# Token halves across the seam between the second mixer and the second MLP, with a multiply moved to GpSimd

## What is computed

```python
h = rms_norm(x, mix_norm_pre)
m = hybrid_mixer(h, ...)                  # ends in concat([attn, rec]) @ w_out
x = x + rms_norm(m, mix_norm_post)        # root over the 1024 features of m, per token
h = rms_norm(x, mlp_norm_pre)
a = relu(h @ w_ff_in)                     # 1024 -> 4096
x = x + rms_norm((a * a) @ w_ff_out, mlp_norm_post)
```

## Time and profile before

| | before |
|---|---|
| median of three executions | 1423.48 us |
| profiled execution, time | 1422.14 us |
| profiled execution, span | 1420.3 us |
| TensorE busy | 1398.5 us, 98% |
| ScalarE busy | 832.2 us, 59% |
| VectorE busy | 698.4 us, 49% |
| GpSimd busy | 202.0 us, 14% |
| granted TensorE clock | 0.999 of full |

### The profile page before, as it was taken

How to read it: one execution, slowest core, us unless ns; L and a number is a source line. 1 busy time by engine, 2 the same in 40 slices (tenths; PEclk the granted TensorE clock), 3 DMA queues, 4 the chain that set the end, 5 groups by cost and what they waited for, 6 DMA issues and landing times.

```text
span 1420.3 us, 18417 instructions
## 1 busy us (share of the span) xinstructions
PE 1398.5 (98%) x6734; PEld 1121.1 (79%) x6734; DVE 698.4 (49%) x1228; ACT 832.2 (59%) x1174; POOL 202.0 (14%) x236
## 2 busy tenths in 40 slices
PE   7999999999999999999999999999999999999998
PEld 5887877777778888888888887777788888888887
DVE  6992477877734455544154165757465301213324
ACT  7536566776755656665365477645756655535442
POOL 1210100100111111111111111010101111111111
PEclk9999999999999999999999999999999999999999
DMA  9996966566579888888878997754667898888873
GB/s 298 221 188 154 233 156 141 132 156 142 115 197 220 193 188 193 187 202 192 214 177 187 214 233 158 160 139 108 145 153 162 193 202 192 190 202 180 206 163 89
DMA packets 82692, 254.76 MB, mean 179 GB/s; under 512 B 16816, under 2 KB 20016, under 8 KB 82608
## 3 DMA queue, kind: packets, MB, share of 16 engines
q0 software_dynamic: 32400, 117.98, 46.2%
q1 hardware_dynamic: 48768, 132.50, 30.9%
q10 hardware_dynamic: 1440, 3.15, 0.6%
HBM read 128.03 MB, written 3.41 MB: 93 GB/s over the span
## 4 chain that ended last, share of the span: by engine, by line
PE 94%; DVE 3%; ACT 2%; issue 0%; DMA 0%; DVEq 0%; ACTq 0%
PE pg L559 27%; PE pg L561 27%; PE pg L560 27%; PE ps L733 2%; PE py L811 1%; PE ps L947 1%; PE ps L957 1%; ACT pairs_r L1241 1%; PE py L967 1%; DVE acc L1558 1%; PE ps L735 0%; ACT kq_raw L1242 0%; PE ps L949 0%; DVE acc L1555 0%; PE px L632 0%
## 5 line engine op out<-in xcount | busy, mean ns | idle before, releaser
L559 PE MATMUL pg<-x_hi,w_hi 128*128 128x512 f32 x1088 | 429.0, 394 | 0.0
L561 PE MATMUL pg<-x_hi,w_lo 128*128 128x512 f32 x1088 | 424.0, 390 | 0.0
L560 PE MATMUL pg<-x_lo,w_hi 128*128 128x512 f32 x1088 | 423.5, 389 | 0.0
L523 POOL DMA_DIRECT2D w_lo<-w_raw x225 | 194.0, 862 | 1186.3 <-ACT w_lo L1080 1134.9
L1079 ACT ACTIVATE w_hi<-w_raw 128x1024 fp32r<-128x1024 f32 x222 | 233.4, 1051 | 100.9 <-PE pg L561 99.8
L559 PEld LDWEIGHTS pg<-x_hi,w_hi 128*128 128x128 f32 x1088 | 204.3, 188 | 43.5 <-issue 1.6
L561 PEld LDWEIGHTS pg<-x_hi,w_lo 128*128 128x128 f32 x1088 | 204.2, 188 | 43.0
L560 PEld LDWEIGHTS pg<-x_lo,w_hi 128*128 128x128 f32 x1088 | 204.4, 188 | 42.5 <-issue 1.0
L1080 ACT ACTIVATE w_lo<-w_raw 128x1024 fp32r<-128x1024 f32 x222 | 232.3, 1046 | 0.0
L559 PE MATMUL pg<-act_hi,w_hi 128*128 128x512 f32 x424 | 165.0, 389 | 0.0
L561 PE MATMUL pg<-act_hi,w_lo 128*128 128x512 f32 x424 | 165.0, 389 | 0.0
(11 more groups left out here) (384 smaller groups left out, 1743.9 us busy)
## 6 DMA issues: line engine op xcount, KB each, us to landing
w_raw<-weights SPq DMA_DIRECT2D x226, 512.0 KB, 4.8
w_lo<-w_raw POOLq DMA_DIRECT2D x225, 512.0 KB, 5.7
kq_rot<-kq_raw SPq DMA_DIRECT2D x64, 64.0 KB, 3.3
hid<-x SPq DMA_DIRECT2D x4, 512.0 KB, 5.4
hid<-x ACTq DMA_DIRECT2D x8, 256.0 KB, 5.3
out<-hid SPq DMA_DIRECT2D x16, 128.0 KB, 1.8
u_dram<-hid SPq DMA_DIRECT2D x4, 256.0 KB, 5.4
pairs<-u_dram SPq DMA_DIRECT2D x8, 128.0 KB, 6.8
```

Of the source, the lines that this page charges most:

```text
L523: pool.dma_start(w_lo[:, s], w_raw[:, s], accum_op=ALU.add).then_inc(lo_in[s], 16)
L559: pe.matmul(bank[:], wh, xh(k), start=n == 0, stop=False)
L560: pe.matmul(bank[:], wh, xl(k), start=False, stop=False)
L561: last = pe.matmul(bank[:], wl, xh(k), start=False, stop=n == len(ks) - 1)
```

## The change

- **out2 6 and 7 in halves.** TensorE makes tokens 0 to 255 of both units, then tokens 256 to 511 of both. The four results go to four places (`mid_bank`). The sum of squares for half 0 is made inside the second half of out2 6.
- **ff 0, 1 and 2 in halves, no double products.** In each half ff 0 and ff 1 go side by side, tile of input by tile of input, so that one tile of input feeds 6 matmuls; then ff 2. The sum for half 1 lies inside the first half of ff 0 and 1.
- **The root is applied by GpSimd**, in place on `acc`, 16 multiplies of 128x256, between its DMA issues; VectorE then needs one instruction for each tile and half for the new residual.
- ScalarE's high parts, its evacuations and the weight copies for ff 2 are put in a new order. The relu of ff 0 to 2 is made in two halves each.

```diff
+            def scaled_by_root(half, tiles):
+                cols = halves[half]
+                pool.wait_ge(rstd_ready, 4 + half)
+                for k in tiles:
+                    pool.tensor_tensor(acc[:, k, cols], acc[:, k, cols], rstd[:, cols], ALU.mult).then_inc(mid_scaled, 1)
             for v in range(11, len(UNITS)):
+                if v == UNIT[("ff", 2)]:
+                    scaled_by_root(0, range(0, 3))
+                if v == UNIT[("ff", 3)]:
+                    scaled_by_root(0, range(3, KT))
+                    scaled_by_root(1, range(0, 4))
+                if v == UNIT[("ff", 4)]:
+                    scaled_by_root(1, range(4, KT))
                 lo(v, v % RING)
...
+            def last_outputs():
+                for half, cols in enumerate(halves):
+                    for m in (6, 7):
+                        s = UNIT[("out2", m)] % RING
+                        if half == 0:
+                            pe.wait_ge(lo_in[s], lows(UNIT[("out2", m)]))
+                            pe.wait_ge(pg_free[TILE[("out2", m)] % 2], TILE[("out2", m)] // 2)
+                        for k in range(KT):
+                            if (half, m) == (1, 6) and k in (1, 3):
+                                mid_sum(0, k // 2)
+                            last = half_products(mid_bank[m][half], s, k, mx2_hi, mx2_lo, cols)
+                        last.then_inc(tile_done if half else mid_full, 1)
+            def first_units():
+                slot = [UNIT[("ff", i)] % RING for i in range(3)]
+                for half, cols in enumerate(halves):
...
+                    for k in range(KT):
+                        if half == 0 and k in (1, 3):
+                            mid_sum(1, k // 2)
+                        pe.wait_ge(xlo_done, SPLIT["norm4"] + KT * half + k + 1)
+                        for i in range(2):
+                            last = half_products(ff_bank[i][half], slot[i], k, x_hi, x_lo, cols)
+                            if half == 1 and k == KT - 1:
+                                last.then_inc(tile_done, 1)
+                    if half == 0:
+                        pe.wait_ge(lo_in[slot[2]], lows(UNIT[("ff", 2)]))
+                        pe.wait_ge(mid_read, 1)
+                    for k in range(KT):
+                        last = half_products(ff_bank[2][half], slot[2], k, x_hi, x_lo, cols)
+                last.then_inc(tile_done, 1)
...
-            for m in range(KT):
+            for m in range(6):
                 ahead(("out2", m))
-                put(act.activation(x_hi[:, m], hid[:, m], ACT.Copy, scale=par("mlp_pre", m)), xhi_done)
                 a = done(("out2", m))
                 square(4, m, a)
-                put(act.activation(a5_hi[:, m], a, ACT.Copy, scale=both[:, m:m + 1]), xhi_done)
                 free(act.activation(acc[:, m], a, ACT.Copy), ("out2", m))
-            inverse_root(4, rstd)
+            ahead(("out2", 6))
+            mid_out(6, 0)
+            mid_out(7, 0)
+            mid_root(0, ("stat", 4))
+            mid_out(6, 1)
+            norm4_hi(0, 0)
+            u = UNIT[("out2", 7)] + RING - 1
+            act.wait_ge(w_landed[u % RING], 16 * (u // RING + 1))
+            act.wait_ge(tile_done, TILES_AFTER[u - RING])
+            act.activation(w_hi[:, u % RING], w_raw[:, u % RING], ACT.Copy)
+            norm4_hi(0, 1)
+            put(act.activation(w_lo[:, u % RING], w_raw[:, u % RING], ACT.Copy, scale=-1.0), hi_done)
+            norm4_hi(0, 2)
+            mid_out(7, 1)
+            norm4_hi(0, 3)
+            norm4_hi(0, 4)
+            mid_root(1, ("stat4", 1))
+            for k in range(5, KT):
+                norm4_hi(0, k)
             ahead(("ff", 0))
...
+            def norm4_res(half, k):
+                cols = halves[half]
+                dve.wait_ge(mid_scaled, KT * half + k + 1)
+                put(stt(hid[:, k, cols], acc[:, k, cols], par("mix_post", k), hid[:, k, cols], ALU.mult, ALU.add), res_done)
...
+            for half in range(2):
+                for k in range(KT):
+                    norm4_res(half, k)
+                    if k > 0:
+                        norm4_lo(half, k - 1)
+                    if (half, k) == (0, 1):
+                        mid_added(1)
+                norm4_lo(half, KT - 1)
```

## The result

The changed kernel takes 1427.16 us (median of 7 runs, 1426.32 to 1429.21) against 1423.30 us before (7 runs, 1423.08 to 1425.09): a ratio of 1.0029 with an interval of 1.0020 to 1.0038. That is 3.9 us slower where 0.8 us faster was forecast. The profiled execution has 1426.55 us and a span of 1424.4 us.

A forecast was written before the change was run, and what follows sets the result against it. TensorE, busy 98% of the span, was taken to bound the kernel. Work -9.3, stalls +3.2, +0.4 and +2.0 gave -3.7; code loading +3.0 made it -0.7 us: median 1422.7 us, range 1419.5 to 1427.2.

The forecast's parts named there:

- a long loading of code: Rival: GpSimd's code load begins while weights stream; 11 us gives +2.8, 12.2 gives +4.0 (1427.5); 0.13 including slow load with contention.
- Work removed and added: TensorE at the seam: 48 matmuls off (10.88 us), five units cut in halves add 1.60; net -9.3 us.
- Loading of code: GpSimd's first multiply: code brought in for 7.5 us from 1037.6, against 4.5 us of slack; +3.0 us.
- The multiply starts right at the root: Sign that the prediction is wrong; it expected GpSimd's first multiply at 1045.1, with the root there at about 1042.1.
- The wait of 2.2 us ahead of ff 0: Sign of the code load: TensorE idle 2.2 us before ff 0's first matmul, first low part at 1047.7.
- R1: Rival: GpSimd's code is there in time (under 4.5 us or loaded at the start); -3.7 us, 1419.8; chance 0.17.
- Stall A: Half 0: ff 2's issue ahead of tiles 3 to 7 in GpSimd's queue, 2.0 us; VectorE's pace afterwards 1.2; together +3.2.
- Stall B: Half 1: its residuals start beside ff 2's half 0, so most are ready; 0.4 us for the last tiles.
- R2: Rival: GpSimd and VectorE take turns at the seam, a multiply up to 1.46 us; +5.6, 1429.1; chance 0.08 in full.
- Stall C: Before ff 3: it needs ff 1's `pg` bank, held until ScalarE's late relu; about 4.9 us against 2.88 of cover: +2.0.
- A count: GpSimd's queue: ff 3's weight issues move behind seven multiplies; costed at nothing, as ff 3 is needed 13 us after its issue.

The follow-up runs named there:

- the filled wait: The changed kernel plus 32 matmuls of 256 columns, results thrown away, in TensorE's wait before tile 2 of half 0; 1426.15 us, 1.0021 of before.

## Why the prediction was wrong

By its own steps, in the order of the sum:

- **The size of the miss.** ff 3 was to gain 0.7 us in the seam and lost 3.06. The median, 1427.16, lies just inside the upper end of the range (1427.2), and that is luck: this end stood for a long loading of code, and no loading was seen.
- **Work removed and added (-9.3).** Right. Matmuls of 256 columns start 0.120 us apart, and nothing behind ff 3 changed.
- **Loading of code (+3.0).** Wrong, and the largest single mistake of reading: the place of MODIFY_POOL_CONFIG (near 1037, found at 1038.3) was right, that it takes 7.5 us was not. It takes none that could be measured. The first multiply started right at the root, at 1043.17; less the 1.02 us by which this execution's seam starts later, that is 1042.15, and the schedule without the load had 1042.12. "The multiply starts right at the root" was a sign of being wrong. The wait of 2.2 us ahead of ff 0 didn't come either. This was the condition of R1, which would have been 1419.8; the error made the forecast slower by 3.0 us and so hid part of the other one.
- **Stall A (+3.2).** The queue order is as described: the issue stands ahead of tile 3. It goes out 0.4 us later than in my schedule (1048.02 less 1.02, against 1046.6), and tile 3 is scaled 0.5 us later (1049.68 less 1.02, against 1048.2). The wait before tile 2 was put at 2.0; it is 4.58. 2.4 of these 2.6 us are what one locked step of VectorE takes over its 0.48. The waits after it, put at 1.2, were 0.92 at 1058.06 and what the low clock cost. This term, with stall B, is the one that failed: I let GpSimd and VectorE each run at the pace it has alone, and put their slowing each other at nothing outside R2.
- **Stall B (+0.4).** It measures 1.38 before half 1 and 1.3 in small waits; behind it stands the second locked step, 3.78 us.
- **Stall C (+2.0).** Right: 1.61 us, and the cause is the one forecast; the line of ff 3's first matmul names no releaser, but moving the copies took 0.9 us off this wait. ScalarE does relu 0, high part, both copies and only then relu 1, which ends at 1077.14, 0.1 us ahead of ff 3:

```profile
1072.59 0.38 ACT L1596 ACTIVATE rel<-pg 128x256 f32<-128x256 f32 x1 [1.41 <-PE ps L885]
1074.07 0.63 ACT L1153 ACTIVATE act_hi<-pairs 128x512 fp32r<-128x512 f32 x1 [0.83 <-DVE pairs L1654]
1074.61 1.04 ACT L1131 ACTIVATE w_hi<-w_raw 128x1024 fp32r<-128x1024 f32 x1
1075.56 1.04 ACT L1132 ACTIVATE w_lo<-w_raw 128x1024 fp32r<-128x1024 f32 x1
1076.77 0.37 ACT L1596 ACTIVATE rel<-ps 128x256 f32<-128x256 f32 x1
```

- **The rival R2 is what happened, at another price.** I had given it 0.08 and a multiply of 1.46 us, twice its own time. Measured, a turn beside the kernel's multiplies costs VectorE about 0.84 us a step, whether fused (0.48 alone) or a plain sum (0.43 alone); beside multiplies of constants both mostly take 0.72. The multiplies start 0.87 us apart instead of 0.70. With these turns and without the lock-out (the kernel with one wait) the seam is 0.6 us longer than before and the time within 0.2%. The other 2.5 us were not in the rival: the lock-out behind an issue.

- **A count.** Between the issues of ff 2 and ff 3 there are nine multiplies and not seven. Nothing came of it: TensorE never waited for ff 3's weights.

**The account.** The forecast for the seam without the load was -3.7, the result +3.06: 6.8 us unforeseen. 2.5 are the lock-out, by the kernel with one wait. 0.5 are the clock, by the filled wait. That leaves 3.8. For the turn-taking I compare the kernel with the multiplies ahead of the issue with my own schedule: with the issue's wait of 2.0 gone too, it should have come to -5.7, and came to -2.05: 3.6 us. This share is worked out and not measured by itself, since no version keeps GpSimd's share of the work and avoids the turns. It is what is left of a schedule, so it also holds whatever else that schedule had wrong, and that the sum comes to 6.6 of 6.8 is no proof of it. In that kernel's trace TensorE waits 3.5 us for low parts in half 0, while the engines take turns, where the schedule had 1.2. But in half 1 GpSimd is done, VectorE makes a tile each 1.04 us at its own pace, and 0.9 us of waits are there all the same. That turns can cost this much is measured in the kernel with multiplies of constants: 3.8 us, in thirteen steps.

Why the tail of the kernel before gave no warning: there VectorE reads one input from SBUF and one from PSUM, and neither engine is slowed (0.51 and 0.729 us). The prediction had seen this difference and still took the price from that row.

**Still open:** what makes one run behind an issue lock VectorE out and another not, why a turn is shorter than the two instructions, and how much of the 3.6 us the turns are.

## What to carry to other kernels

Before giving GpSimd a share of elementwise work, look at what VectorE does at the same time: with two inputs in SBUF on both sides, price both engines' steps at the turn (here 0.84 instead of 0.48 and 0.73 us), and take their durations only from rows with the same sources. Put such a run ahead of a DMA issue in GpSimd's queue, and not straight behind one; if it must be behind, one wait for the completion of its first instruction is cheap (here it gave 2.5 us of the seam). And a median landing time is no bound: a DMA with a median of 5.7 us took 8.42 once, and 7.3 us of slack didn't cover it.

## What the runs showed of the hardware that was not expected

- Multiplies of GpSimd straight behind a DMA issue had overlapping records (1.03 us long, 0.68 us apart) and held a VectorE step of 0.48 us for 2.88, 3.12 and 3.78 us, until the last of them was done. With one completion wait it was 0.98 and 1.74 us. The filled kernel repeated it (2.95 and 3.79 us). Of the two such runs on constants one did so.
- Runs of 3, 4 and 8 multiplies not behind an issue took turns with VectorE, 0.83 to 0.87 us for most of its steps, fused or plain, with the multiplies 0.87 us apart. Alone the two take 0.48 and 0.70 us, so a turn is shorter than their sum.
- The first tensor_tensor of the program started 0.10 us after its MODIFY_POOL_CONFIG.
- After 4.4 us of idle TensorE resumed at a granted clock of 0.99 (1053.24 to 1053.90), and then had 0.50 for 3.4 us. It fell for as long beginning within an idle of 2.87 us in the kernel where each multiply waits, and behind five waits with 0.6 to 1.4 us of idle each (1048 to 1057) in the one with multiplies of constants. Filled with matmuls, the same stretch kept 1.00. It was worth 0.5 us of the seam.
